# A hybrid decoder step on one core: the order of depthwise taps, index sums and index chunks, and two K products less in the threshold search

## The reference, cut to what matters

```python
# indexer: which 256 keys a query attends
s     = einsum('thd,ld->thl', qi, ki) * 64 ** -0.5
score = einsum('th,thl->tl', wi * 8 ** -0.5, relu(s))      # 8 index heads
score = where(k_pos <= q_pos, score, -inf)
idx   = top_k(score, 256)
# convolution branch
c = depthwise_conv(u, dw_w, width 31) + dw_b               # u = glu_a * sigmoid(glu_b)
conv = silu(layer_norm(c))
# both branches, gated, through one output projection
y = x + concat(attn * silu(gate_a), conv * silu(gate_c)) @ w_out
```

## Time and profile before

| | us |
|---|---|
| median of 3 runs (1017.45 to 1022.96) | 1021.0 |
| the profiled execution | 1022.88 |
| its span, first to last instruction | 1021.0 |
| TensorE busy | 918.9 (90%) |
| VectorE busy | 690.4 (68%) |
| ScalarE busy | 348.6 (34%) |
| index stage, from the first cached score in it to the first count | 261.68 to 363.74 |
| threshold search, to its last group sum | 363.74 to 515.97 |

### The profile page before, as it was taken

How to read it: one execution, slowest core, us unless ns; L and a number is a source line. 1 busy time by engine, 2 the same in 40 slices (tenths; PEclk the granted TensorE clock), 3 DMA queues, 4 the chain that set the end, 5 groups by cost and what they waited for, 6 DMA issues and landing times.

```text
span 1021.0 us, 11394 instructions
## 1 busy us (share of the span) xinstructions
PE 918.9 (90%) x3952; PEld 508.5 (50%) x3952; DVE 690.4 (68%) x1532; ACT 348.6 (34%) x750; POOL 84.4 (8%) x89
## 2 busy tenths in 40 slices
PE   3999999999988679999969898797697889999998
PEld 2866666664332236666534244453465555445432
DVE  4218999998587788888898888956587564332101
ACT  6311101101344568888600000313855363321000
POOL 0120112001133000000000000001011010310000
PEclk9899999999999979999989799798799799999999
DMA  8272011213255050020030000005021111321111
GB/s 298 92 206 27 1 47 39 84 47 119 83 167 168 16 177 30 1 83 1 0 103 32 11 31 1 1 1 214 21 64 52 32 35 39 124 83 41 64 63 43
DMA packets 35459, 69.90 MB, mean 68 GB/s; under 512 B 9625, under 2 KB 12097, under 8 KB 35393
## 3 DMA queue, kind: packets, MB, share of 16 engines
q1 hardware_dynamic: 28233, 43.99, 13.3%
q0 software_dynamic: 7168, 25.17, 7.6%
HBM read 58.52 MB, written 11.11 MB: 68 GB/s over the span
## 4 chain that ended last, share of the span: by engine, by line
PE 78%; DVE 13%; ACT 3%; issue 3%; DMA 1%; SPq 1%; DVEq 0%; POOL 0%; ACTq 0%; POOLq 0%
PE ps L529 74%; PE ps L532 5%; DVE SC L1392 2%; DVE ct L1314 1%; DMA xn<-in_x_prompt 1%; DVE pv L1570 1%; ACT PTs L1018 1%; DVE eqm L1420 1%; ACT uT L1191 1%; DVE LB L1571 1%; DVE uT L1776 0%; ACT relu L1122 0%; ACT sqj L1031 0%; DVE junk L1420 0%; DVE zN L1594 0%
## 5 line engine op out<-in xcount | busy, mean ns | idle before, releaser
L529 PE MATMUL ps<-xT,W 128*128 128x344 f32 x960 | 286.9, 457 | 0.0
L529 PEld LDWEIGHTS ps<-xT,W 128*128 128x128 f32 x960 | 180.9, 191 | 90.8 <-issue 3.5
L529 PE MATMUL ps<-W,xT 128*128 128x512 f32 (+3 forms) x576 | 224.8, 546 | 0.0
L1340 DVE SCALAR_TENSOR_TENSOR ctmp<-uT,chw,ctmp 128x1024 f32<-128x1024 f32 x116 | 153.0, 1319 | 4.0
L529 PEld LDWEIGHTS ps<-W,xT 128*128 128x128 f32 (+1 forms) x576 | 95.8, 188 | 114.4 <-issue 113.8
L1159 ACT ACTIVATE sgj<-SC,cand,sense 128x1024 bf16<-128x1024 f32 (+2 forms) x96 | 104.4, 1088 | 25.8 <-DVE cand L1474 20.8
L1018 ACT ACTIVATE PTs<-ps 128x512 f32<-128x512 f32 (+3 forms) x96 | 43.0, 483 | 128.2 <-PE ps L532 123.5
L1807 DVE TENSOR_TENSOR ps<-ps,TP 128x256 f32<-128x256 f32 (+1 forms) x64 | 26.4, 412 | 69.4 <-PE ps L529 69.0
L1204 ACT ACTIVATE nsq<-ps 128x512 f32<-128x512 f32 (+1 forms) x18 | 10.7, 596 | 163.2 <-DVE nss L1583 115.8
L532 PE MATMUL ps<-Cc,Pm 128*128 128x128 f32 x288 | 47.3, 304 | 17.6 <-ACT PTs L1018 17.0
L529 PE MATMUL ps<-W,uT 128*128 128x512 f32 x128 | 60.1, 613 | 0.0
(11 more groups left out here) (309 smaller groups left out, 1007.6 us busy)
## 6 DMA issues: line engine op xcount, KB each, us to landing
W<-in_w_in SPq DMA_DIRECT2D x8, 2048.0 KB, 8.9
xn<-in_x_prompt SPq DMA_DIRECT2D x8, 512.0 KB, 7.7
W<-in_w_out SPq DMA_DIRECT2D x1, 4096.0 KB, 13.7
resid<-in_x_prompt SPq DMA_DIRECT2D x16, 256.0 KB
out<-resid SPq DMA_DIRECT2D x16, 256.0 KB
out<-V SPq DMA_DIRECT2D x8, 256.0 KB
out<-zN SPq DMA_DIRECT2D x8, 256.0 KB, 2.0
bias_rows<-tprow SPq DMA_DIRECT2D x1, 1536.0 KB
```

The lines of the kernel that those rows point to most:

```text
L529: return nc.tensor.matmul(out, lhsT, rhs, start=start, stop=stop)
L1340: ins = vec.scalar_tensor_tensor(conv[:, c, :] if j == CW - 1 else acc_, src, chw[:, c, j:j + 1], acc_, ALU.mult, ALU.add)
```

## The change

The taps are put in the order of a list, `TAPS`: 19 of channel chunk 0 alone, then one of chunk 0 and one of chunk 1 in turns, then 1 and 2, then 2 and 3, and the last 19 of chunk 3 alone. Each tap waits only for the tap that wrote its accumulator. The sums get a list too, `SUMS`: for blocks 4 to 7 the two column chunks of a head pair are taken in turns (first head of both, second head of both), and each sum waits for the last sum on its own columns; ScalarE's relus follow the same order. The slots are replaced by a stream: five V products, cached scores 0 and 1, two chunks, cached score 2, and then six times half a V product and six chunks, with a cached score behind chunks 7, 13, 19, 25 and 31 (`TURN_AT`), and two chunks more. VectorE does its cached turns in front of the sums of chunks 0, 6, 12, 18, 24 and 30 (`TURN_BEFORE`). `sc16b` moves to the gate's region. `K_EARLY` goes from 4 to 2, so that two K products leave the search and `COLUMNS_PER_SUM` falls from 2472 to 2238.

```diff
--- before.py
+++ after.py
@@ -213,7 +213,7 @@
     tprow = sb("tprow", [H, FW], F32, rV)
     sqj = sb("sqj", [P, D], F32, rV + 12288)
     relu = sb("relu", [P, 4, 512], F32, rTP)
-    sc16 = [sb("sc16a", [16, 32, 2, 16], F32, rKV), sb("sc16b", [16, 32, 2, 16], F32, rSC + 12800)]
+    sc16 = [sb("sc16a", [16, 32, 2, 16], F32, rKV), sb("sc16b", [16, 32, 2, 16], F32, rGC)]
     uT = sb("uT", [P, 4, CW - 1 + SEQ], F32, rU)
     conv = uT[:, :, CW - 1:CW - 1 + SEQ]
     oneh = sb("oneh", [NBK, FW], F32, rSC)
@@ -443,25 +443,21 @@
         i, hp, a = CHUNKS[n]
         return min(512, (i + 1) * P - a)
 
-    FIRST_SLOT, SLOTS = 5, NT + 1
-    CACHED_AT = {1: (0,), 4: (1,), 5: (2, 3), 6: (4, 5), 7: (6, 7)}
-    def chunks_in(s):
-        last = sum(1 for x in CHUNKS if x[0] < NT - 1)
-        if s == SLOTS - 1:
-            return range(last, len(CHUNKS))
-        k, n = s - FIRST_SLOT, SLOTS - 1 - FIRST_SLOT
-        return range(max(k, 0) * last // n, max(k + 1, 0) * last // n)
-    def cached_in(s):
-        return CACHED_AT.get(s, ())
-    def halves(s):
-        c = chunks_in(s)
-        return c[:len(c) // 2], c[len(c) // 2:]
+    V_AHEAD = 5
+    def sums_order():
+        order, n = [], 0
+        while n < len(CHUNKS):
+            two = CHUNKS[n][0] >= 4
+            order += [(n, 0), (n + 1, 0), (n, 1), (n + 1, 1)] if two else [(n, 0), (n, 1)]
+            n += 2 if two else 1
+        return order
+    SUMS = sums_order()
+    TURN_AT = {2 + 6 * j: 2 + j for j in range(6)}
+    TURN_BEFORE = {6 * j: 2 + j for j in range(6)}
 
     EVACUATED_EARLY = NT
 
@@ -474,6 +470,19 @@
 
     DVE_CHUNKS = [0, 1, 2, 3]
     NTAP = len(DVE_CHUNKS) * CW
+    ALONE = 19
+    def tap_order():
+        order, at_ = [(0, j) for j in range(ALONE)], [ALONE, 0, 0, 0]
+        for c in range(3):
+            while at_[c] < CW:
+                order += [(c, at_[c]), (c + 1, at_[c + 1])]
+                at_[c] += 1
+                at_[c + 1] += 1
+        return order + [(3, j) for j in range(at_[3], CW)]
+    TAPS = tap_order()
 
 
     K_FROM = 2
@@ -488,7 +497,7 @@
 
     Y_ADD = [Y_FROM + (8 * u + 7) // Y_RATE + 1 for u in range(YEARLY)]
 
-    K_EARLY = 4
+    K_EARLY = 2
     STAGE_UNITS = DURING_SEARCH[EVACUATED_EARLY:] + [("k", t) for t in range(K_EARLY)]
 
     def columns_of(g):
@@ -712,25 +721,33 @@
                 r = slice(64 * e, 64 * e + 64)
                 mm(pt(("ix", n, e))[:, 0:width(n)], qiT[r, hp, i * P:(i + 1) * P], kiT[r, a:a + width(n)]).then_inc(plan.fill_sem(("ix", n, e)), 1)
 
-        for s in range(SLOTS):
-            one, two = halves(s)
-            def between():
-                for n in one:
-                    index_scores(n)
-            if s < NT:
-                natural("v", s, 2, between)
-            else:
-                between()
-            if s == 0:
+        for t in range(V_AHEAD):
+            natural("v", t, 2)
+            if t == 0:
                 own_score()
-            for n in cached_in(s)[:1]:
-                cached(n)
-            for n in two:
+            if t == 1:
+                cached(0)
+        cached(1)
+        def stream(lo, hi):
+            for n in range(lo, hi):
                 index_scores(n)
-            for n in cached_in(s)[1:]:
-                cached(n)
+                if n + 1 in TURN_AT:
+                    cached(TURN_AT[n + 1])
+        done = [0]
+        def half_turn():
+            stream(done[0], done[0] + 6)
+            done[0] += 6
+        stream(0, 2)
+        done[0] = 2
+        for t in range(V_AHEAD, NT):
+            natural("v", t, 2, half_turn)
+            half_turn()
+        stream(done[0], len(CHUNKS))
         for g, m in STAGE_UNITS:
             if g in TRANSPOSED:
                 transposed(g, m, paced=True)
@@ -1111,11 +1128,11 @@
             if n == 7:
                 scores_out(7)
 
-        def index_relu(n):
-            for e in range(2):
+        def index_relu(lo, hi):
+            for u in range(lo, hi):
+                n, e = SUMS[u]
                 tag = ("ix", n, e)
-                u = 2 * n + e
                 act.wait_ge(*plan.full(tag))
                 if u >= 4:
                     act.wait_ge(relu_used, u - 3)
@@ -1136,21 +1153,24 @@
                 piece_out(g, m, gaT[:, m // 3, a:a + n], sT[:, 2], ACT.Silu)
             if g == "gc":
                 a, n = piece_rows(m)
+                if m == 0:
+                    act.wait_ge(scd_out[1], 128)
                 piece_out(g, m, gcT[:, m // 3, a:a + n], sT[:, 3], ACT.Silu)
 
 
-        for s in range(SLOTS):
-            one, two = halves(s)
-            for n in one:
-                index_relu(n)
-            if s < NT:
-                evacuate("v", s)
-            for n in cached_in(s)[:1]:
-                cached_out(n)
-            for n in two:
-                index_relu(n)
-            for n in cached_in(s)[1:]:
-                cached_out(n)
+        for t in range(V_AHEAD):
+            evacuate("v", t)
+            if t == 1:
+                cached_out(0)
+        cached_out(1)
+        for n in range(len(CHUNKS)):
+            if n % 2:
+                index_relu(2 * n - 2, 2 * n + 2)
+            if n + 1 in TURN_AT:
+                cached_out(TURN_AT[n + 1])
+            t = V_AHEAD + (n - 7) // 12
+            if n % 12 == 7 and t < NT:
+                evacuate("v", t)
         ev = EVACUATED_EARLY
         for r in range(BITS + 1):
             act.wait_ge(cand_ready, r + 1)
@@ -1318,19 +1338,21 @@
 
         def taps(lo, hi):
             for m in range(lo, hi):
-                c, j = DVE_CHUNKS[m // CW], m % CW
+                c, j = TAPS[m]
                 if m == 0:
                     v.wait_ge(uzero_done, 1)
                     v.wait_ge(*plan.drained("chw"))
                     v.wait_ge(ki_stored, 32)
                 if j == 0:
                     v.wait_ge(u_done, 3 * c + 3)
+                    if c >= 2:
+                        v.wait_ge(taps_done, TAPS.index((c - 2, CW - 1)) + 1)
                 src = uT[:, c, j:j + SEQ]
-                acc_ = ctmp[:, m // CW % 2, :]
+                acc_ = ctmp[:, c % 2, :]
                 if j == 0:
                     ins = vec.tensor_scalar(acc_, src, chw[:, c, 0:1], chw[:, c, CW:CW + 1], ALU.mult, ALU.add)
                 else:
-                    v.wait_ge(taps_done, m)
+                    v.wait_ge(taps_done, TAPS.index((c, j - 1)) + 1)
                     if j == CW - 1:
 
                         if c < 3:
@@ -1376,32 +1398,28 @@
         cached_turn(1)
         taps(NTAP - 8, NTAP)
 
-        def weighted(n):
+        def weighted(u):
+            n, e = SUMS[u]
             i, hp, a = CHUNKS[n]
-            if (i, hp, a) == (NT - 1, 0, 0):
-                v.wait_ge(scd_out[1], 128)
-            for e in range(2):
-                u, h = 2 * n + e, 2 * hp + e
-                src, dst = relu[:, u % 4, 0:width(n)], sc(i)[:, a:a + width(n)]
-                v.wait_ge(*plan.drained(("ix", n, e)))
-                if h == 0:
-                    vec.tensor_scalar(dst, src, wI[:, i, 0:1], None, ALU.mult).then_inc(relu_used, 1)
-                else:
-                    v.wait_ge(relu_used, u)
-                    vec.scalar_tensor_tensor(dst, src, wI[:, i, h:h + 1], dst, ALU.mult, ALU.add).then_inc(relu_used, 1)
-        for s in range(FIRST_SLOT, SLOTS):
-            one, two = halves(s)
-            for n in cached_in(s)[:1]:
-                cached_turn(n)
-            for n in one:
-                weighted(n)
-            for n in cached_in(s)[1:]:
-                cached_turn(n)
-            for n in two:
-                weighted(n)
+            h = 2 * hp + e
+            src, dst = relu[:, u % 4, 0:width(n)], sc(i)[:, a:a + width(n)]
+            v.wait_ge(*plan.drained(("ix", n, e)))
+            if h == 0:
+                vec.tensor_scalar(dst, src, wI[:, i, 0:1], None, ALU.mult).then_inc(relu_used, 1)
+                return
+            for w in range(u):
+                if CHUNKS[SUMS[w][0]][0::2] == (i, a):
+                    last = w
+            v.wait_ge(relu_used, last + 1)
+            vec.scalar_tensor_tensor(dst, src, wI[:, i, h:h + 1], dst, ALU.mult, ALU.add).then_inc(relu_used, 1)
+        for n in range(len(CHUNKS)):
+            if n in TURN_BEFORE:
+                cached_turn(TURN_BEFORE[n])
+            if n % 2 == 0:
+                for u in range(2 * n, 2 * n + 4):
+                    weighted(u)
 
         rows = [sc(i) for i in ACT_BLOCKS + DVE_BLOCKS] + [SD[:, :]]
         v.wait_ge(sd_in, 16)
```

## The result

The kernel after the change takes 1033.01 us (median of 12 runs, 1024.29 to 1035.29) against 1020.86 us (12 runs, 1017.45 to 1032.26): a ratio of 1.0094, 95% interval 1.0059 to 1.0129. It is slower, by 12 us in the medians; 1034.5 had been forecast, in a range of 1012 to 1046. The profiled execution took 1035.29 us with a span of 1033.5.

What follows compares the result with a forecast made beforehand. TensorE's queue order was taken to set the time, VectorE counting only where TensorE waits for it. The stream's +16.3 and -2.5 from rounds and offset made +13.8 us: 1034.5 us forecast, range 1012 to 1046.

Steps and rivals of the forecast that it cites:

- Taps: Taps in turns free 10 us of VectorE, all lost waiting for the own-key score: cost 0.
- Sums: Index stage: independent 512-column sums step by 0.67 instead of 0.855 us, saving 12 us of VectorE; arrival depends on the stream.
- The stream: Index stage's new order makes VectorE idle after each transpose turn; search starts at 380 instead of 363.74 us: +16.3 us.
- the tail behind the turn: After each transpose turn: last score quarter 1.79, weighting 0.95, half product 3.63, chunk to relu 1.16, relu to sum 0.62; together 8.15.
- rival B: Index stage: waits real but half as long, half product under the score's tail or more sums ready; 1016 to 1026 us, chance 0.08.
- Rounds: Threshold search: two K products leave, so a round takes 3.98 instead of 4.38 us; 30 rounds give -12 us.
- Rival D: Search rounds stay at about 4.4 us, set by VectorE or ScalarE's evacuations; 1045 us, chance 0.06.
- The offset: Behind the search, two moved K products delay the equal counts' offset; VectorE waits 10.3 us: cost +10.
- The 0.5 us of clock: After the offset, less TensorE idling might speed the next product: -0.5 us counted, bounds 0 and -1.8.
- Steps 4 and 5: Shorter search rounds and the later equal-count offset together: -2.5 us, between -5 and +3.
- Rival C: Independent operations step no faster than dependent ones, so sums in turns save nothing; 1042 us, chance 0.07.
- four ready sums: Index stage: after a transpose turn VectorE has only four sums (2.7 us) ready, then idles some 5.4 us each half turn.

Runs made afterwards that it cites:

- experiment 4: Kernel before with only the taps in turns: 1021.44 us, ratio 1.0013; kernel before with only sums in turns, slots evened and sc16b moved: 1011.43 us.
- Experiment 5: Changed kernel with sums in plain order: 1027.49 us; with cached scores also two chunks later: 1001.77 us; that with every sum waiting for the previous: 1008.87 us.
- experiment 1: Changed kernel with K_EARLY back at 4: 1028.97 us; kernel before with only K_EARLY set to 2: 1020.34 us.
- Experiment 2: Changed kernel with each cached-key score of the stream two chunks later on TensorE, VectorE's order kept: 1002.88 us, ratio 0.9836.

## Why the prediction was right

1. **Taps, 0 us:** right. The wait for the own score grew from 3.84 to 13.59 us (14 forecast), and experiment 4 gives 1.0013. Seven taps in turns started (8.44 - 1.28) / 6 = 1.19 us apart (1.20 forecast).
2. **Sums, 0.855 to 0.67 us:** the sizes were right. Experiment 5 has 0.855 and the mean of both, 0.77; two independent sums stand in after at 364.04 us, 1.41 - 0.75 = 0.66 apart. What I did not see is that the narrower wait alone would free half of the steps, and that in block 7 the banks would hold the other half.
3. **The stream, +16.3 us:** the mechanism was right and its size too large by 3.9 us. The mis-sized term is the tail behind the turn. I had put the last quarter of the score (1.79) and the weighting (0.95) one behind the other, 2.74 us. The 1.79 is the row of a whole score whose transposes were ready, and a last quarter alone took nearly as long (302.94 to 304.58, 1.64). The weighting ran beside it (302.86 and 303.29) and added nothing, so 1.88 remained. The five chains from turn to sum are 6.99, 7.57, 7.30, 7.32 and 7.31, 36.5 us instead of 5 x 8.15 = 40.8; rival B has an overlap of this kind, but with the half product, and waits half as long, which did not come. The sums between took 24.5 us instead of 25.4. Against it the last chain was longer: 9.8 us from the end of the last turn (352.88) to its first sum instead of about 9.1 (7.3 and 1.16 + 0.62), since the last weighting waited 1.49 us for ScalarE. A pair took 3.22 us, as forecast (3.2).
4. **Rounds, -12 us:** right, -12.3, at 3.98 us a round. Rival D is out.
5. **The offset, +10 us:** VectorE waited 11.71 us for it instead of 10.3. Of the three products in front of it 6.8 us fell at half clock, of the one product before 3.4, and I had counted the two more at full clock (windows of TensorE's clock, after and then before):

```profile
515.40:522.20 6.80, 6.12 (x9) 2.95 (x10) 6.66 (x18) 0.00 (x0) 0.00 (x0) 0.50 0.00 0
```
```profile
517.20:520.60 3.40, 3.40 (x6) 1.34 (x5) 3.40 (x9) 0.00 (x0) 0.00 (x0) 0.50 0.00 0
```

   With `K_EARLY` 2 on the kernel before, where the three products ran at full clock, the wait was 8.65 us (experiment 1). The 0.5 us of clock that I had hoped for behind it did not come: the product there took 9.95 us again, as in the earlier trace rows. Steps 4 and 5 together were -0.5 in place of -2.5 us.

The forecast of the span, +13.8, came out as +12.5: 3.9 too much up to the first count (4.4 in the stage, less 0.5 by which it began later), 2.0 too little in steps 4 and 5, and 0.6 behind 710 us that I had at nothing. Part of the closeness is thus errors of opposite sign.

Rival C did not come: a step that waits for the one before costs 1.32 us against 1.19 at 1024 columns and 0.855 against 0.66 at 512, and making every step wait again moved the first count by 4.1 us, 3.4 of it behind the stage's start. The rule that the prediction quotes with it from the Trainium skill, page "VectorE: DVE Perf Modes", section "The DRAIN you can't avoid", does not hold for these operations by these numbers. The same section adds that an operation that is not held starts earlier, which the prediction left out.

The forecast hung on whether four ready sums or more stand behind a turn. That was read from the order of TensorE's queue and not from busy times, which looked as if VectorE could stream. Experiment 2 shows that it was the right question.

## What to carry to other kernels

When two engines serve each other in turns (transposes one way, chunks the other), count how much ready work the waiting engine has at the point where the other must wait for it, and place the consumer of the slow turn as many units later as it takes; here two chunks decided 26 us. An in-order queue charges everything moved in front of a small, wanted instruction, and moving that one forward passes the charge to the next. Before operations are interleaved to hide a dependence, narrow the wait to what the operation really reads: the order may then have most of the free steps already.

## What the runs showed of the hardware

- TensorE fell to the lower of its two clocks (1.2 GHz; granted 0.50) at gaps of only 2 to 3 us: for 3.4 us from 283.3 us on in after, behind a wait of 2.09 us for a transpose (first row below), and for 6.8 us from 515.4 on, in a gap of 3.28 us. Not every such gap brings it: behind the same gap of 3.28 us in experiment 1 (505.09) the granted clock was 1.00 up to 526 us.
- The clock spreads equal work. The stage from 710.60 us to the end of after took 322.90 us at a mean granted clock of 0.93; the same instructions in the version with `K_EARLY` 4 took 318.52 us at 0.94 (last row). The runs of after fall into 1024.29 to 1026.53 (4 of 12) and 1032.38 to 1035.29 (8), so differences of 4 us between two single runs say nothing.

```profile
283.30:286.70 3.40, 3.40 (x12) 1.41 (x13) 3.40 (x4) 0.00 (x0) 2.57 (x3) 0.51 0.43 114
...
710.60:1033.50 322.90, 288.99 (x1586) 157.11 (x1586) 141.89 (x341) 107.70 (x251) 32.08 (x32) 0.93 0.19 64
```
```profile
708.88:1027.40 318.52, 285.31 (x1586) 154.40 (x1586) 141.87 (x341) 107.61 (x251) 32.06 (x32) 0.94 0.20 65
```

What is open: why attention draws the one or the other; the small rest of 0.6 us is inside that spread.
